# Second mixer: differential v ahead of the dilated panels, another order of head steps, turns and evacuations, and narrower waits of two output products

## The reference, cut to what matters

```python
def mixer_dilated_differential(h, w_in, ..., w_out, cos128, sin128, cos64, sin64, lambda_init):
    cq, ck, cv, dq, dk, dv = split_cols(h @ w_in, IN1_SPLITS)     # 6 x 512 columns
    cq, ck = rope128(cq) * 128 ** -0.5, rope128(ck)
    o_c = dilated_attention(cq, ck, cv)                           # 4 heads of 128
    q1, q2, k1, k2 = rope64(dq[..., 0]), rope64(dq[..., 1]), rope64(dk[..., 0]), rope64(dk[..., 1])
    o_d = differential_attention(q1, q2, k1, k2, dv, lam)         # 4 heads, two score maps each
    o_d = rmsnorm(o_d, diff_norm) * (1.0 - lambda_init)
    return concatenate([o_c, o_d]) @ w_out
```

## Time and profile before

| | us |
|---|---|
| median of three runs | 1543.81 (1542.79 to 1544.06) |
| the profiled execution | 1543.93 |
| its span in the trace | 1542.0 |
| busy: PE, PEld, DVE, ACT, POOL | 1498.4, 1344.4, 1170.6, 764.2, 99.9 |
| projection `in1` from panel 3's end to the output product | 772.7 to 855.8 of the trace |
| output product `out1` | 855.8 to about 879 |

### The profile page before, as it was taken

One profiled execution on the slowest core, in us unless ns is written; L12 is line 12 of the kernel. 1 busy time (PEld: TensorE's weight loads), 2 busy tenths in 40 slices (PEclk: granted clock), 3 DMA queues, 4 the chain that ended last, 5 costly groups with the idle time before them and its releaser, 6 DMA issues.

```text
span 1542.0 us, 23913 instructions
## 1 busy us (share of the span) xinstructions
PE 1498.4 (97%) x9958; PEld 1344.4 (87%) x9958; DVE 1170.6 (76%) x1390; ACT 764.2 (50%) x935; POOL 99.9 (6%) x70
## 2 busy tenths in 40 slices
PE   7999999999999999999998999999999989999988
PEld 6888899988888888888987888888999869999967
DVE  7878768756887778787677688777779677589774
ACT  5433456445433453334545543345564674555662
POOL 2000010011000010000100100001213001003000
PEclk9999999999999999999999999999999999999999
DMA  7555535213655555555441365554444214634302
GB/s 269 213 194 191 166 139 188 83 56 149 222 186 197 181 174 208 185 178 206 169 163 57 135 218 191 188 177 168 178 164 141 108 54 167 216 137 162 112 28 82
DMA packets 51888, 246.76 MB, mean 160 GB/s; under 512 B 4619, under 2 KB 5771, under 8 KB 27718
## 3 DMA queue, kind: packets, MB, share of 16 engines
q1 hardware_dynamic: 50662, 238.29, 43.9%
q0 software_dynamic: 1120, 6.96, 1.2%
HBM read 244.18 MB, written 1.05 MB: 159 GB/s over the span
## 4 chain that ended last, share of the span: by engine, by line
PE 80%; DVE 10%; ACT 6%; issue 2%; DMA 0%; POOL 0%; SPq 0%; DVEq 0%; ACTq 0%
PE ps L1149 21%; PE ps L1151 10%; PE ps L1072 9%; PE ps L1074 9%; PE ps L1073 9%; PE ps L1202 8%; PE ps L1203 4%; PE ps L1359 4%; ACT w_hi L1613 2%; DVE w_lo L1939 1%; ACT work L1826 1%; PE ps L1507 1%; PE ps L1496 1%; DVE act_two L2047 1%; ACT act_two L1691 1%
## 5 line engine op out<-in xcount | busy, mean ns | idle before, releaser
L1613 ACT ACTIVATE w_hi<-raw 128x2048 fp32r<-128x2048 f32 x186 | 355.2, 1913 | 387.1 <-PE ps L1151 270.5
L1939 DVE TENSOR_TENSOR w_lo<-raw,w_hi 128x2048 fp32r<-128x2048 f32 x179 | 409.6, 2291 | 138.8 <-ACT w_hi L1613 136.4
L1149 PE MATMUL ps<-act_two,w_hi 128*128 128x512 f32 x1408 | 445.2, 398 | 2.6 <-DVE xn L1948 1.3
L1072 PE MATMUL ps<-act_two,w_hi 128*128 128x256 f32 x1088 | 319.2, 293 | 4.0 <-DVE act_two L2186 2.9
L1151 PEld LDWEIGHTS ps<-act_two,w_lo 128*128 128x128 f32 x1408 | 265.8, 189 | 63.2
L1074 PE MATMUL ps<-act_two,w_lo 128*128 128x256 f32 x1088 | 307.7, 283 | 0.0
L1073 PE MATMUL ps<-act_two,w_hi 128*128 128x256 f32 x1088 | 307.7, 283 | 0.0
L1151 PE MATMUL ps<-act_two,w_lo 128*128 128x256 f32 x1408 | 277.9, 279 | 0.0
L1149 PEld LDWEIGHTS ps<-act_two,w_hi 128*128 128x128 f32 x1408 | 215.6, 190 | 5.4 <-DVE xn L1948 1.7
L1072 PEld LDWEIGHTS ps<-act_two,w_hi 128*128 128x128 f32 x1088 | 208.5, 192 | 9.6 <-issue 5.6
L1073 PEld LDWEIGHTS ps<-act_two,w_hi 128*128 128x128 f32 x1088 | 208.6, 192 | 4.4 <-issue 4.3
(11 more groups left out here) (294 smaller groups left out, 2063.7 us busy)
## 6 DMA issues: line engine op xcount, KB each, us to landing
raw<-panels SPq DMA_DIRECT2D x184, 1024.0 KB, 4.8
raw<-panels SPq DMA_DIRECT2D x80, 512.0 KB, 4.9
raw<-panels SPq DMA_DIRECT2D x8, 256.0 KB, 5.8
table<-tab POOLq DMA_DIRECT2D x1, 1472.0 KB, 9.0
table<-tab POOLq DMA_DIRECT2D x1, 1216.0 KB, 5.5
xn<-x_in SPq DMA_DIRECT2D x4, 256.0 KB, 4.8
work<-mem_in POOLq DMA_DIRECT2D x1, 1024.0 KB, 9.4
xn<-mem_in POOLq DMA_DIRECT2D x1, 1024.0 KB, 5.0
```

Source lines behind the costliest of these rows:

```text
L1072: pe.matmul(o, l[0], r[0], start=start, stop=False, skip_group_check=shared)
L1149: pe.matmul(grid(ps[:, bank + half], 2), w[half][0], act_two[:, slots[c]], start=c == 0, stop=False)
L1613: nc.scalar.activation(w_hi[:, s], raw[:, s], ACT.Copy).then_inc(panel_hi, 1)
L1939: tt(w_lo[:, s], raw[:, s], w_hi[:, s].bitcast(F32), ALU.subtract).then_inc(panel_lo, 1)
```

## The change

1. `in1` gets another order: dq, dk (0 to 3), dv (4, 5), cq, ck (6 to 9), cv (10, 11). `IN1_SOURCE` lets the loads take the panels in that order; `dest` and the turns' waits are renumbered.
2. Panel 4 comes straight behind panel 3, the turns `r64b` 0 and 2 behind it. The other six turns go into rounds 0 to 3, behind the head steps of the round. `r128` turns use banks 3 and 7, not 6 and 7.
3. The halves of panels 6 to 11, twelve, go to rounds 0, 0, 0, 1, 1, 1, 2, 2, 3, 4, 5, 6.
4. In this weave an evacuation stands directly behind its half panel (`AT_ONCE`); only the splits stay behind the next round's steps.
5. The differential heads run staggered as before. The dilated heads run in pairs: scores of 0 and 1 in round 4, their mask_max and exp in 5, scores of 2 and 3 with divide, turn_p and p_cols of 0 and 1 in 6, and so on to attend of 2 and 3 in round 9. `cn_sq` of both norm groups is in round 6, `cn_sum` and `cn_rstd` in 7, `cn_use` in 8, `gate_out` of the first dilated group in 9.
6. `turn_p` of differential heads uses bank 2 alone, so it waits for p_cols of the head before.
7. Each panel of `out0` and `out1` waits for the one group that it reads. Pieces of `out0`'s panel 0 that overwrite banks of the norm wait for that norm's reader.

```diff
+AT_ONCE = [("act", "evacuate", ("in1", k)) for k in range(6, 12)]
...
             out.append(first)
+            if rest and rest[0] in AT_ONCE:
+                out.append(rest.pop(0))
...
-BESIDE_1 = [0, 0, 1, 1, 2, 3, 4, 5]
+BESIDE_1 = [0, 0, 0, 1, 1, 1, 2, 2, 3, 4, 5, 6]
+IN1_SOURCE = [0, 1, 2, 3, 8, 9, 4, 5, 6, 7, 10, 11]
...
-    out += weave(rounds(ROPE, [("r64b", g) for g in (0, 2, 1, 3)]), panel_list("in1", None, 4, 8), range(4))
-    ropes = [[(e, k, (("r128", g),)) for g in pair for e, k, _ in ROPE] for pair in ((0, 2), (1, 3))]
-    heads = rounds(SCORES_FIRST, [("dif", h) for h in range(4)] + [("dil", h) for h in range(4)])
+    turn = lambda name, *gs: [(e, k, ((name, g),)) for g in gs for e, k, _ in ROPE]
+    out += weave([[], turn("r64b", 0, 2)], panel_list("in1", None, 4, 6), [0, 1])
+    turns = [turn("r64b", 1), turn("r64b", 3) + turn("r128", 0), turn("r128", 1), turn("r128", 2, 3)]
+    heads = rounds(SCORES_FIRST, [("dif", h) for h in range(4)])
+    two = lambda p, *steps: [(e, k, (("dil", h),)) for e, k in steps for h in (2 * p, 2 * p + 1)]
+    dilated = [[]] * 4 + [two(0, ("pe", "scores")), two(0, ("dve", "mask_max"), ("act", "exp")),
+                          two(1, ("pe", "scores")) + two(0, ("dve", "divide"), ("pe", "turn_p"), ("act", "p_cols")),
+                          two(0, ("pe", "attend")) + two(1, ("dve", "mask_max"), ("act", "exp")),
+                          two(1, ("dve", "divide"), ("pe", "turn_p"), ("act", "p_cols")), two(1, ("pe", "attend"))]
     pair = lambda *steps: [(e, k, (("fo", g),)) for e, k in steps for g in (0, 1)]
-    norms = [pair(("act", "cn_sq")), pair(("pe", "cn_sum"), ("act", "cn_rstd"), ("dve", "cn_use"))]
-    out += weave(merge(ropes, heads, [[]] * 7 + norms, [[]] * 9 + [[("dve", "gate_out", (("dil", 0),))]]),
-                 halves(panel_list("in1", None, 8)), BESIDE_1)
+    norms = [pair(("act", "cn_sq")), pair(("pe", "cn_sum"), ("act", "cn_rstd")), pair(("dve", "cn_use")), [("dve", "gate_out", (("dil", 0),))]]
+    out += weave(merge(heads, dilated, turns, [[]] * 6 + norms), halves(panel_list("in1", None, 6)), BESIDE_1)
...
+        def turn_bank(unit):
+            return 2 if unit[0] == "dif" else 2 + att_index[unit] % 2
...
-                    last = {("out0", 0): ("cn_use", ("ro", 1)), ("out0", 2): ("cn_use", ("do", 1)), ("out1", 0): ("cn_use", ("fo", 1)), ("out1", 2): ("gate_out", ("dil", 1))}
+                    last = {("out0", 0): ("cn_use", ("ro", 0)), ("out0", 1): ("cn_use", ("ro", 1)), ("out0", 2): ("cn_use", ("do", 0)), ("out0", 3): ("cn_use", ("do", 1)),
+                            ("out1", 0): ("cn_use", ("fo", 0)), ("out1", 1): ("cn_use", ("fo", 1)), ("out1", 2): ("gate_out", ("dil", 0)), ("out1", 3): ("gate_out", ("dil", 1))}
+                    if name == "out0" and k == 0 and pieces[-1] >= 2:
+                        pe.wait_ge(act_done, at("act", "cn_rstd", ("ro", 1)))
+                    if name == "out0" and k == 0 and pieces[-1] >= 4:
+                        pe.wait_ge(dve_done, at("dve", "cn_use", ("ro", 1)))
+                    if (name, k) == ("out1", 0):
+                        pe.wait_ge(act_done, at("act", "cn_rstd", ("fo", 1)))
...
-                if i >= 2:
-                    pe.wait_ge(act_done, at("act", "p_cols", att_list[i - 2]))
+                ago = 1 if unit[0] == "dif" or i and att_list[i - 1][0] == "dif" else 2
+                if i >= ago:
+                    pe.wait_ge(act_done, at("act", "p_cols", att_list[i - ago]))
```

More of the change, by code:

```diff
@@ L758, in build @@
         for g in range(4):
-            ropes["r128", g] = (cqk[:, 2 * g:2 * g + 2], tab(2, "swap128"), tab(2, "cos128"), tab(2, "sin128"), 6 + g // 2,
-                                evac("in1", 4 + g))
+            ropes["r128", g] = (cqk[:, 2 * g:2 * g + 2], tab(2, "swap128"), tab(2, "cos128"), tab(2, "sin128"), (3, 7)[g % 2],
+                                evac("in1", 6 + g))
             ropes["r64b", g] = (dqk[:, 2 * g:2 * g + 2], tab(2, "swap64"), tab(2, "cos64"), tab(2, "sin64"), 6 + g // 2,
@@ L845, in build @@
             dest["in0", 12 + k] = (rows(rv, k), "rows", ACT.Copy)
-            dest["in1", 8 + k] = (rows(dv, k), "rows", ACT.Copy)
+            dest["in1", 4 + k] = (rows(dv, k), "rows", ACT.Copy)
             dest["in1", 10 + k] = (rows(cv, k), "rows", ACT.Copy)
@@ L857, in build @@
             dest["in1", k] = (blocks(dqk, k), "cols", ACT.Copy)
-            dest["in1", 4 + k] = (blocks(cqk, k), "cols", ACT.Copy)
+            dest["in1", 6 + k] = (blocks(cqk, k), "cols", ACT.Copy)
             for l in range(2):
@@ L1007, in load_panel @@
                         source = b + (n - b + 2) % 4
+                    if b == BASE["in1"]:
+                        source = b + IN1_SOURCE[n - b]
                     if b in (BASE["in2_0"], BASE["in2_1"]) and n - b < 4:
@@ L1527, in turn_p @@
                 pe.wait_ge(dve_done, at("dve", "divide", unit))
-                if i >= 2:
-                    pe.wait_ge(act_done, at("act", "p_cols", att_list[i - 2]))
-                p, bank = probs[:, i % 2, 0], ps[:, 2 + i % 2]
+                ago = 1 if unit[0] == "dif" or i and att_list[i - 1][0] == "dif" else 2
+                if i >= ago:
+                    pe.wait_ge(act_done, at("act", "p_cols", att_list[i - ago]))
+                p, bank = probs[:, i % 2, 0], ps[:, turn_bank(unit)]
                 second = SEQ if full else P
@@ L1836, in p_cols @@
                 n = 512 if full else 384
-                nc.scalar.activation(p_t[:, i % 2, 0:n], ps[:, 2 + i % 2, 0:n], ACT.Copy).then_inc(act_done, 1)
+                nc.scalar.activation(p_t[:, i % 2, 0:n], ps[:, turn_bank(unit), 0:n], ACT.Copy).then_inc(act_done, 1)
             def y_hi(l, b):
```

## The result

| | before | after |
|---|---|---|
| median of the runs (4 each) | 1543.93 us (1542.79 to 1545.42) | 1533.05 us (1532.76 to 1534.09) |
| ratio, 95% interval | | 0.9927 (0.9914 to 0.994) |
| span of the profiled execution | 1542.0 | 1531.3 |

What follows compares the result with a forecast made beforehand. TensorE's products hold 80% of the chain, but the heads before out1 are a latency chain over three engines. 1543.93 less 9.9 (earlier out1) and 1.4 (out0) gives 1532.6, taken as 1532.5 us; range 1529.5 to 1537.0.

Steps and rivals of the forecast that it cites:

- The count of products against the stretch: From the heads' begin to the output product, PE's counted work is 42.1 of 56.0 us, so 13.9 are no work.
- PE's busy share: In the same stretch PE is busy 46.62 of 56.00 us, which would make the loss 9.4 us.
- The walk: Layer 1's mixer stepped through in the new order with trace durations: out1 starts at 845.9 instead of 855.79, 9.9 us less.
- the four waits: PE's waits in layer 1's mixer: scores of dil 0 0.95, attend of dil 0 0.9, turn_p of dil 3 0.7, attend of dil 2 0.85.
- the wait at the first dil scores: Round 4 of layer 1's mixer: PE waits 0.95 us at scores of dil 0 for VectorE's last turn.
- out0: Layer 0's output product: its first piece no longer waits 1.38 for cn_use of ro 1; 1.4 us less, bounds 0 and 1.4.
- The sum: Whole kernel: 1543.93 - 9.9 - 1.4 = 1532.6 us, put at 1532.5 for the median.
- The clock: Rival, chance 0.18: half clock comes again in the new tail, under output panels, costing 1.7 us: 1534.2.
- VectorE as the bound: Rival, chance 0.14: VectorE, nearly without gap from 788.9 to 824.4, delays the tail by 3.5 us: 1536.0.
- ScalarE's queue as a block: Rival, chance 0.03: evacuations at once hold up exps and high splits in ScalarE's queue, up to 17.3 us: 1549.8.
- The change doing less than it says: Rival, chance 0.11: the tail stays an equally long latency chain; only out0 and waits beside panels, 4 to 5 us, saved: 1538.5.
- The price of 1.2 us for the evacuation at once: Tail of layer 1's mixer: panel 11's evacuation stands ahead of exp of dil 2 and 3, costing some 1.2 us.

Runs made afterwards that it cites:

- a_all: Changed kernel with a_tail's edits and a_scores_late's together: 1530.14 us, ratio 0.9914 to the kernel before.
- a_out0_old: Changed kernel with out0's waits as before the change: 1534.76 us.
- b_waits: Kernel before with only part 7 added, each panel of out0 and out1 waiting for the one group it reads: 1540.08 us, ratio 0.9979.
- a_scores_late: Changed kernel with scores of dilated heads 0 and 1 behind round 4's half panel instead of ahead of it: 1532.5 us.
- a_once_11: Changed kernel with evacuations of panels 8, 9 and 10 no longer directly behind their panels, that of 11 still so: 1535.0 us.
- a_turns_first: Changed kernel with each round's turns ahead of its head steps, as before the change: 1538.16 us.
- a_single: Changed kernel with the dilated heads staggered one by one instead of in pairs: 1534.46 us.
- a_tail: Changed kernel with both norm sums ahead of attend of dil 0, and panel 11's evacuation behind exp of dil 2 and 3: 1532.66 us, ratio 0.9923.

## Why the prediction was right, point by point

**What bounds.** The count of products against the stretch said 13.9 us, PE's busy share 9.4. The stage has by now given 9.22 with the change and 12.40 with a_all, without one product less; 1.6 of either is the half clock of the tail before, which the count has in its 13.9 too. By order and waits alone a_all has 10.8, so the busy share would have been too small an estimate of what is there.

**The walk** named the four waits. Their sizes were 0.95, 0.9, 0.7 and 0.85, and 1.37, 1.02, 0.27 and 1.05 measured: right in sum within 0.3, and the third by more than half too long. Panel 3's last product starts 1.55 earlier in the new trace (771.07), so the walk's times minus 1.55 are to be compared with PE's timeline:

| | walk | measured |
|---|---|---|
| scores of dif 0, round 0 | 784.65 | 784.51 |
| scores of dif 1, round 1 | 795.15 | 795.05 |
| scores of dif 2, round 2 | 806.45 | 806.46 |
| scores of dif 3, round 3 | 814.45 | 814.40 |
| turn_p of dif 2, round 4 | 820.95 | 820.90 |
| scores of dil 0 | 822.90 | 823.41 |
| attend of dil 0 | 837.75 | 838.22 |
| output product | 844.35 | 845.01 |

It holds within 0.15 for four rounds and then loses 0.5 at one step, the scores of dil 0. VectorE's last turn was later than the walk had it, for a wait that I had left out: mask_max of a head writes the buffer of the head two before, so it also waits for that head's turn_p, which stands behind the scores on PE. It shows in round 2 (808.01, after 1.04 of idle time) and in round 3, where it decides:

```profile
815.96 0.29 DVE L2254 CUSTOM_DVE_ANT_0 work<-ps,table 128x128 f32<-128x128 f32 x1 [0.33 <-PE ps L1563]
```

From here to the end of the last turn are a mask_max, a divide and two turns, 1.23 + 1.86 + 4.34 = 7.43, which gives 823.39. The walk has that end at 824.4, that is 822.85 here, and so this mask_max at 815.4. The 0.5 goes through to the end, where it is 0.66. Less this 0.5 to 0.7, the term is 9.2 to 9.4 and not 9.9; measured 9.2 by the stage. So the step that was mis-sized is the wait at the first dil scores, 0.95 in the walk and 1.37 in the trace.

**out0.** 1.4 was forecast, 1.60 to 1.65 measured. The step that was mis-sized is the reading of the bracket, as a_out0_old shows.

**The sum.** 9.9 + 1.4 = 11.3; measured 9.22 + 1.60 = 10.8, and 10.9 between the medians. The two misses have opposite signs, 0.7 too much and 0.2 too little. The 9.9 holds the 1.7 of the half clock as well: the walk ran at full clock from a trace that had a fall, and there it had luck on its side as far as the fall belongs to the execution.

**The rivals.** The clock did not fall in the new mixer, in either profiled execution of the changed kernel, and in none of the tails built on it. That shorter waits are the reason is not shown. Its price of 1.7 was nearly right where PE is the bound, 1.6, but b_waits shows that it is not a constant: it was 0 at 822. VectorE as the bound: it did hold the first dil scores, 1.37 and not 0.95, but a_scores_late and a_all show that PE has other work for that time. ScalarE's queue as a block: not in this order, a_once_11; but a_turns_first shows the mechanism at work as soon as an exp comes late. The change doing less than it says did not come true: the tail is shorter, and a_single shows that the pairs are a part of that.

**What was wrong in it.** The price of 1.2 us for the evacuation at once. It was in the text and not in the sum, as the walk carried the right chain: both cn_rstd, then p_cols. Such a price does exist once the norm sums are out of the way, 1.48 by a_tail.

## What to carry to other kernels

Where engines run fixed lists, a change of order can be priced by walking all lists at once with durations from the trace: here within 0.7 us of 9.9. What went wrong was a wait that was left out, that for a buffer's earlier reader, and, by five microseconds, looking at one engine's list alone. A step moved on one engine is paid for by what is queued behind its reader on the next, and two moves can each be worthless or harmful and good together. Cut the span into stages at rows that all kernels share: the two changed stages repeat within 0.05 us here, where the times of whole runs of one kernel differ by more than one. And look at the granted clock of both traces before a difference is put down to the code.

## What the runs showed of the hardware that was not expected

The stretch of half clock inside layer 1's mixer, 3.4 us long each time, comes after short waits of PE, none over 2.4 us: it starts at 846.6 before, at 822 in b_waits, at 827.5 in a_turns_first, and is nowhere in the changed kernel's mixer. The same waits ahead of it brought a fall in one execution and none in another (1.49 and 0.82 ahead of 822 in b_waits and of 825 before), so the waits alone do not decide. Where PE waits for another engine anyway it cost nothing (11.25 us with it and without), and where PE is the bound 1.6. And the bracketed idle time of PE is about 0.25 us less than what taking the wait away gives back, 1.38 against 1.61 to 1.65, since it counts from the end of a pipelined row.
